# Expert weights of a two-layer transformer step pass through twelve SBUF buffers in place of six

## The reference, cut to what matters

```
glog = x @ w_rg; gsel = argmax(glog)                 # one of 4 groups for each token
elog_g = (x @ w_re) of the group gsel                # 4 experts in a group
top_p, top_i = top_k(softmax(elog_g), 2)             # two experts of the group, renormalised
hid = silu(x @ w_g[e]) * (x @ w_u[e])                # D_EXPERT = 256
y   = sum_e gate[e] * hid[e] @ w_d[e]
```

## Time and profile before

| | |
|---|---|
| median of 3 runs | 1904.09 us (1903.96 to 1904.28) |
| profiled execution, its own time | 1903.26 us |
| its span in the profile | 1901.7 us |
| PE busy | 1690.2 us, 89% of the span |
| DVE, ACT, POOL busy | 1015.7, 874.1, 663.5 us |
| transfers | 360.07 MB, mean 189 GB/s |
| experts of layer 0, from the first split after routing to the last unit's | 714 to 937 us |
| experts of layer 1 | 1648 to 1872 us |

### The profile page before, as it was taken

One profiled execution on the slowest core, in us unless ns is written; L12 is line 12 of the kernel. 1 busy time (PEld: TensorE's weight loads), 2 busy tenths in 40 slices (PEclk: granted clock), 3 DMA queues, 4 the chain that ended last, 5 costly groups with the idle time before them and its releaser, 6 DMA issues. The chain is left out here.

```text
span 1901.7 us, 30317 instructions
## 1 busy us (share of the span) xinstructions
PE 1690.2 (89%) x9817; PEld 1352.0 (71%) x9817; DVE 1015.7 (53%) x1807; ACT 874.1 (46%) x1493; POOL 663.5 (35%) x425
## 2 busy tenths in 40 slices
PE   3799998999999979999739999989999998899994
PEld 2588786776878757777627887867768786677773
DVE  0314437665432158899632263475634502789895
ACT  0343333534443337777513332444444333477773
POOL 1454453333456621000114444533334666101001
PEclk8899999999999989999969999999999999899997
DMA  7622243332556328999872222323344553399994
GB/s 272 221 97 84 91 137 100 106 123 106 184 199 234 111 78 328 374 362 358 313 270 90 89 98 94 128 93 108 114 170 173 208 197 110 128 362 363 362 362 179
DMA packets 117036, 360.07 MB, mean 189 GB/s; under 512 B 11740, under 2 KB 31772, under 8 KB 116896
## 3 DMA queue, kind: packets, MB, share of 16 engines
q1 hardware_dynamic: 92656, 320.23, 46.9%
q0 software_dynamic: 5760, 21.02, 2.9%
q10 hardware_dynamic: 18480, 17.08, 2.8%
HBM read 337.51 MB, written 20.77 MB: 188 GB/s over the span
## 5 line engine op out<-in xcount | busy, mean ns | idle before, releaser
L664 POOL TENSOR_TENSOR wlo<-raw,whi 128x1024 fp32r<-128x1024 f32 x204 | 491.6, 2415 | 621.1 <-ACT whi L810 621.0
L1124 PE MATMUL G<-whi,hhi 128*128 128x512 f32 (+1 forms) x1440 | 580.4, 403 | 21.6 <-ACT pB L899 7.4
L1126 PE MATMUL G<-whi,hlo 128*128 128x512 f32 (+1 forms) x1440 | 560.8, 389 | 0.0
L1125 PE MATMUL G<-wlo,hhi 128*128 128x512 f32 (+1 forms) x1440 | 560.5, 389 | 0.0
L1528 DVE TENSOR_TENSOR wlo<-raw,whi 128x1024 fp32r<-128x1024 f32 x288 | 344.7, 1222 | 44.1 <-ACT whi L818 39.9
L818 ACT ACTIVATE whi<-raw 128x1024 fp32r<-128x1024 f32 x288 | 304.4, 1060 | 91.0 <-PE S L1126 32.8
L1124 PEld LDWEIGHTS G<-whi,hhi 128*128 128x128 f32 x1440 | 273.2, 190 | 100.0 <-DVE wlo L1528 23.8
L1126 PEld LDWEIGHTS G<-whi,hlo 128*128 128x128 f32 x1440 | 272.7, 189 | 58.4
L1125 PEld LDWEIGHTS G<-wlo,hhi 128*128 128x128 f32 x1440 | 273.6, 190 | 48.8
L810 ACT ACTIVATE whi<-raw 128x1024 fp32r<-128x1024 f32 x204 | 213.5, 1054 | 176.4 <-PE G L1126 97.0
L1143 PE MATMUL O<-raw,cond 128*32 128x128 f32 x1536 | 59.7, 320 | 55.1 <-DMA raw<-in_units 45.1
(11 more groups left out here) (301 smaller groups left out, 2190.5 us busy)
## 6 DMA issues: line engine op xcount, KB each, us to landing
raw<-in_units SPq DMA_DIRECT2D x588, 512.0 KB, 5.2
y_sorted<-yo POOLq DMA_DIRECT2D x12, 512.0 KB, 7.1
hs<-h_sorted POOLq DMA_DIRECT2D x10, 514.0 KB, 7.5
bias<-in_nat_bias ACTq DMA_DIRECT2D x16, 256.0 KB, 3.2
h_sorted<-sig POOLq DMA_DIRECT2D x6, 514.0 KB, 13.2
x_scratch<-pA SPq DMA_DIRECT2D x2, 1536.0 KB, 13.1
pA<-x_scratch ACTq DMA_DIRECT2D x2, 1536.0 KB, 9.8
pC<-g_scratch ACTq DMA_DIRECT2D x4, 512.0 KB, 8.4
```

The source lines that it names most:

```text
L664: lo_done.of(nc.gpsimd.tensor_tensor(wlo[:, k, :], raw[:, POS_OF[g] % RAW, :], whi[:, k, :].bitcast(F32), ALU.subtract))
L1124: nc.tensor.matmul(dst, st_hi, mv_hi, start=start, stop=False)
L1125: nc.tensor.matmul(dst, st_hi, mv_lo, start=False, stop=False)
L1126: return nc.tensor.matmul(dst, st_lo, mv_hi, start=False, stop=stop)
```

## The change

The experts' units pass through a ring of twelve buffers (`RING = 2 * RAW`). Six of them are new views of memory that is there already: three of `yacc` and three of `pB` (list `more`). Unit n of a tile goes to buffer n % 12: 0 to 5 are the views, 6 to 11 the six of `raw`. The views have semaphores of their own (`w_more`). ACT and DVE read a unit through `expert_raw(n)`; their order and that of PE and POOL are as before. The loads ahead of the experts are now twelve: units 0 to 2 into `yacc` when the last users of that memory are done, units 6 to 11 into `raw` as it comes free, units 3 to 5 into `pB` after the last transpose of the second norm (`nt_pe`). `load_gate` follows them. From then on SP waits for `e_lo` of unit n and issues unit n+12. The projections' stream keeps its six buffers.

```
+RING = 2 * RAW
...
+        more = [yacc[:, t, :] for t in range(TILES)]
+        more += [pB[:, :, :, :].rearrange("p a t n -> p (a t n)")[:, (1 + i) * D:(2 + i) * D] for i in range(TILES)]
...
+        w_more = [sg(f"w_more{i}", 16) for i in range(RING - RAW)]
...
+        def expert_raw(n):
+            r = n % RING
+            return more[r] if r < RAW else raw[:, r - RAW, :]
...
-                        for r in range(RAW):
-                            released(len(STREAM) - RAW + r)
-                            expert_load(r, 0)
+                        need(kv_out["D"], 1)
+                        sp.wait_ge(*tp_pe.at(l, TP_NO["D", "k", 3]))
+                        sp.wait_ge(*mt_pe.at(l, 3))
+                        for n in range(TILES):
+                            expert_load(n, 0)
+                        for r in range(RAW):
+                            released(len(STREAM) - RAW + r)
+                            expert_load(RAW + r, RAW)
+                        need(nt_pe, 2 * KD - 1)
+                        for n in range(TILES, RAW):
+                            expert_load(n, 0)
                         need(*evacuated(CHUNK_NO["wout", 1], TILES - 1))
                         sp.wait_ge(*g_out.at(l, 1))
                         load_gate(sp, 1)
...
                         with sp.Fori(0, GRP - 1) as i:
                             for k in range(UT // RAW):
-                                next_block(i, k, i * UT + RAW * (k + 1))
+                                next_block(i, k, i * UT + RAW * (k + 2))
...
-                    hi_done.of(nc.scalar.activation(whi[:, n % CONV, :], raw[:, n % RAW, :], ACT.Copy))
+                    hi_done.of(nc.scalar.activation(whi[:, n % CONV, :], expert_raw(n), ACT.Copy))
...
-                    e_lo.of(tt(wlo[:, n % CONV, :], raw[:, n % RAW, :], whi[:, n % CONV, :].bitcast(F32), ALU.subtract))
+                    e_lo.of(tt(wlo[:, n % CONV, :], expert_raw(n), whi[:, n % CONV, :].bitcast(F32), ALU.subtract))
```

More of the change, by code:

```diff
@@ L188 @@
 RAW = 6
+RING = 2 * RAW
 CONV = 3
 NBLOCK = OVER * UT // RAW
-assert UT % RAW == 0 and len(STREAM) % RAW == 0 and NG % CONV == 0 and UT % CONV == 0
+assert UT % RING == 0 and len(STREAM) % RAW == 0 and NG % CONV == 0 and UT % CONV == 0
 POS_OF = [p for p, s in enumerate(STREAM) if s[0] == "gemm"]
@@ L329, in program @@
         gact = sig[:, :, :].rearrange("p t n -> p (t n)")[:, TILES * DEXP:].rearrange("p (t n) -> p t n", t=TILES)
+        more = [yacc[:, t, :] for t in range(TILES)]
+        more += [pB[:, :, :, :].rearrange("p a t n -> p (a t n)")[:, (1 + i) * D:(2 + i) * D] for i in range(TILES)]
+        assert len(more) == RING - RAW
         def row(name, lo=0, hi=None):
@@ L581, in _, with expert_load @@
                     elif s == ("experts",):
-                        def expert_load(r, block):
-                            w_in[r].of(sp.dma_start(
-                                raw[:, r, :], a["units"][bass.ds(block + (l * NU + len(STREAM) + r), 1), :, :]
+                        def expert_load(n, block):
+                            r = n % RING
+                            w = w_more[r] if r < RAW else w_in[r - RAW]
+                            w.of(sp.dma_start(
+                                expert_raw(n), a["units"][bass.ds(block + (l * NU + len(STREAM) + n % RAW), 1), :, :]
                                 .rearrange("a p n -> p (a n)")))
@@ L598, in next_block @@
                         def next_block(i, k, block):
-                            for r in range(RAW):
-                                sp.wait_ge(*e_lo.in_tile(l, i, UT, k * RAW + r))
-                                expert_load(r, block)
+                            for n in range(k * RAW, (k + 1) * RAW):
+                                sp.wait_ge(*e_lo.in_tile(l, i, UT, n))
+                                expert_load(n, block)
                         with sp.Fori(0, GRP - 1) as i:
                             for k in range(UT // RAW):
-                                next_block(i, k, i * UT + RAW * (k + 1))
+                                next_block(i, k, i * UT + RAW * (k + 2))
                         need(gidx_dve, UT // RAW - 1)
-                        for k in range(UT // RAW - 1):
-                            next_block(GRP - 1, k, (GRP - 1) * UT + RAW * (k + 1))
+                        for k in range(UT // RAW - 2):
+                            next_block(GRP - 1, k, (GRP - 1) * UT + RAW * (k + 2))
                         for i in range(GRP, NT):
@@ L611, in _ @@
                                 block = block_at((i - GRP) * (UT // RAW) + k)
-                                if k:
-                                    next_block(i, k - 1, block)
-                                else:
-                                    next_block(i - 1, UT // RAW - 1, block)
-                        for r in range(RAW):
-                            w_in[r].n += (GRP - 2) * (UT // RAW)
+                                if k >= 2:
+                                    next_block(i, k - 2, block)
+                                else:
+                                    next_block(i - 1, UT // RAW - 2 + k, block)
+                        for w in w_in + w_more:
+                            w.n += (GRP - 2) * (UT // RING)
             sp.wait_ge(layer_end.handle, DEPTH + 1)
@@ L812, in high @@
                 def high(i, n):
[L814 to L816 removed]
+                    r = n % RING
+                    w, first = (w_more[r], 0) if r < RAW else (w_in[r - RAW], len(STREAM) // RAW)
+                    act.wait_ge(w.handle, w.value(l, first + n // RING) + i * (16 * (UT // RING)))
                     act.wait_ge(*e_unit.in_tile(l, i, UT, n - CONV))
[L818 removed]
+                    hi_done.of(nc.scalar.activation(whi[:, n % CONV, :], expert_raw(n), ACT.Copy))
                 def rows_high(hf, i):
```

## The result

| | before | after |
|---|---|---|
| median of the runs, same chip | 1904.03 us (4 runs, 1902.29 to 1904.28) | 1884.3 us (4 runs, 1881.35 to 1887.94) |
| ratio, 95% interval | | 0.9919 [0.9894, 0.9943] |
| span of the profiled execution | 1901.7 us | 1886.4 us |
| predicted | | 1891 us, range 1883 to 1898 |

The change makes the kernel faster, by 11 to 20 us of 1904 in this comparison. The ratio is an estimate over all runs with their scatter, not the quotient of the two medians (which is 0.9896 here). Measured again on two other chips the ratio was 0.9931 and 0.9923. So 13 to 15 us is the better figure: single runs of the kernel before lie up to 13 us from their median on those chips, and four runs place a median badly.

The account below looks back on a forecast made before the run. PE was taken to set the pace, with transfers late only at times; 8.5 us in the experts plus 4.5 between the layers, 13.0 off 1903.26, gave 1890.3, plus 0.8 for the runs' median: 1891 us, range 1883 to 1898.

Parts of the forecast that it names:

- the boundary: From layer 0's last expert loads to the layer's end: 3.5 us from the write plus 1.0 from the gather, 4.5 us.
- the DMA row's 9: Profile's DMA share during the experts: looks transfer-bound, but the prediction said transfers have some 10% to spare on average.
- the term 16.1 - 12 x 0.63 = 8.5 us: Experts, both layers: PE's 16.1 us of waits less 0.63 us that stays in each of twelve tiles; gain 8.5 us.
- The bound of 16.1 us: Experts, both layers: the most that better supply could give, if all of PE's waits go.
- The prediction's check of 8.5 us against the tile: Experts: 8.5 us over twelve tiles is 0.7 us each, bringing the mean tile to about 36.6 us.
- I take the whole difference, 3.5 us: End of layer 0: POOL's wait for the last result's write falls from 5.92 us to layer 1's 2.43.
- another 1.0 us: Gather at the end of layer 0: 1.0 us gained of the 3.3 us by which it exceeds layer 1's.
- The bound of 5.1 us: Between the layers: the most to be had, since PE's modulation group ends 5.1 us before DVE's last add.
- All waits gone: Rival: all of PE's waits in the experts and all of the boundary go, 21.2 us, giving 1883 us; chance 0.12.
- Little reaches the end: Rival: supply improves, but DVE's backlog halves the experts' gain or the boundary gives nothing; 1896 to 1900 us, chance 0.15.
- The change doesn't do what it says: Rival: units are late because of when buffers come free, not how many; nothing moves, 1904 us, chance 0.06.
- Slower by a deeper queue: Rival: in each layer's first tile POOL's hs read stands behind more loads, the turn waits 10 us; 1911 us, chance 0.05.

Follow-up runs that it names:

- norows: Kernel before (six buffers) with POOL's row transfers of a tile made small, output not the reference's; ratio 0.9931, median 1886.5 us beside 1899.7.
- ring8: Changed kernel with a ring of eight buffers in place of twelve; ratio to the kernel before 0.9936, median 1885.4 us beside 1897.6.
- nohead: Changed kernel, twelve buffers, but only six loads before the experts begin; ratio to the kernel before 0.9956, median 1889.1 us beside 1897.6.
- swap: Changed kernel with the ring's halves in the other order, units 0 to 5 in the old buffers; ratio to the kernel before 0.9907, median 1883.7 us.
- again2: The changed kernel measured a third time, nothing altered; ratio to the kernel before 0.9923, median 1882.1 us beside 1895.2.
- again: The changed kernel measured once more, nothing altered; ratio to the kernel before 0.9931, median 1884.9 us beside 1897.6.
- jump: Changed kernel, but a layer's last expert load waits for unit 17, not unit 11; ratio to the kernel before 0.9933, median 1883.1 us.
- bparams: Kernel before (six buffers) with SP's layer-end wait moved from the parameters' loads to the copy of x; ratio 0.9975, median 1892.6 us beside 1895.2.

## Why the prediction was right, and where its terms were off

The forecast (1886 to 1896 us, 1891) has the right sign and size: the ratios 0.9919, 0.9931 and 0.9923, applied to 1904, give 1889 to 1891, and the median on the first chip, 1884.3, is within the range of 1883 to 1898, though below the 1886. Two terms were off, in opposite directions: the experts gave 13.8 us where I had 8.5, the boundary 1.9 to 2.8 where I had 4.5. That 1891 came so close is partly luck, since these errors cancel in part, and the stages together (about 16 us) show more than the whole does (13 to 15).

*Cause in the experts: right.* The late units of the earlier trace rows came from POOL's row transfers meeting a ring of six. norows shows it from one side and ring8 and nohead from the other. That the DMA row's 9 is no bound was right as well: from 718 to 752 us, most of the first tile of the changed kernel and the start of the second, the queues moved

```profile
DMA packets 3746, 13.69 MB, mean 403 GB/s; under 512 B 414, under 2 KB 414, under 8 KB 3742
```

where a whole tile of before went at 349 to 373. The 358 GB/s of the Trainium skill (DMA: Bandwidth & Descriptors, section Bandwidth) are passed here too, over 34 us; the same section gives that figure for both cores of an HBM pair streaming at once, and this kernel runs on one core.

*Size in the experts: the term 16.1 - 12 x 0.63 = 8.5 us was undersized; 13.8 measured.* Two parts, which the traces show and no run tested alone. First, what stays is less than 7.6 us: PE's waits are 5.0 us in the 18 places of the four rows above, and ten of these, 3.0 us, are the wait for elo behind the turning of the hidden rows. The gain in waits as shown is 16.1 - 5.0 = 11.1 us. Second, a wait costs more than its row shows. On PE's timeline of the changed kernel:

```profile
853.31 0.39 PE L1146 MATMUL S<-wlo,ehi 128*128 128x512 f32 x1
853.53 0.39 PE L1147 MATMUL S<-whi,elo 128*128 128x512 f32 x1
854.24 0.49 PE L1145 MATMUL S<-whi,ehi 128*128 128x512 f32 x1 [0.32 <-DVE elo L1549]
```

Matmuls follow each other at about 0.23 us, but each is drawn 0.39 us long, since its end is modelled. The third starts 0.71 us behind the second, 0.48 us later than at that pace, and the row shows 0.32. So 0.16 us of each wait is drawn as busy time. Before had 33 such places, after 18: 15 x 0.16 = 2.4 us. 11.1 + 2.4 = 13.5 us, against 13.8 measured. Added up from start to start over these places the delays are 21.2 us before and 7.8 after, which is nearly the same difference. The bound of 16.1 us that I gave for this stretch left that out and should have been 16.1 + 33 x 0.16 = 21.4.

The prediction's check of 8.5 us against the tile hid this. The tile came out as it said, 36.6 us, but the two tiles of the earlier trace rows were short ones: behind the first tile, from fourth unit to fourth unit, the tiles of before took 37.0 to 37.5 us in layer 0 and 37.4 to 38.8 in layer 1.

*First tile.* From its fourth unit to the next tile's it takes 40.4 us before and 37.5 after in layer 0, 39.4 and 37.5 in layer 1. So 4.8 of the 13.8 us are in the two first tiles. The prediction spread the gain evenly over twelve. Without the head start (nohead) they take 41.2 and 39.3 us, so the length of the ring gives nothing there and this share is the head start's.

*Between the layers: 4.5 us predicted.* The order of events came as said: the modulation loads start at 920.00, right behind DVE's split of unit 18 on its timeline,

```profile
918.60 1.22 DVE L1549 TENSOR_TENSOR wlo<-raw,whi 128x1024 fp32r<-128x1024 f32 x1
```

at 918.60 + 1.22 = 919.8. They start 10.7 us ahead of the write, before it was 6.6. The write's wait fell from 5.92 to 3.07 to 3.86 us, where I took 2.4. To the end of the layer 2.4 to 3.2 us were gained, to the copy of x 1.9 to 2.8. So the term was oversized by some 2 us, and its cause is only half right. The failed step is "I take the whole difference, 3.5 us": 2.1 to 2.9 us of it came. The gather, for which I took another 1.0 us, went from 15.8 us behind the write's end to between 14.7 and 16.3 in the three profiles, from 1.1 gained to 0.5 lost. I had added the two as if they were independent. The profiles point to a trade between them. Behind the first six modulation loads four more are issued as PE uses up the first ones, and the earlier they are issued, the longer the gather takes, with small exceptions. No run moved these four alone, so this is a reading and not shown as a cause. The seven kernels with a longer ring and the parameters' wait in place, by the issue of these four against the write and the gather's length, are:

| us | swap | again2 | nohead | ring8 | after | again | jump |
|---|---|---|---|---|---|---|---|
| four loads issued behind the write | 3.6 | 4.2 | 4.2 | 4.3 | 6.9 | 7.2 | 7.9 |
| gather, first issue to last sum | 16.1 | 15.7 | 16.1 | 15.6 | 14.5 | 14.1 | 13.1 |

So the write and the gather together take 19.1 to 21.0 us in them, whatever the order of the loads was.

What stays open is the 22.3 us of the kernel before (22.9 in bparams). It issues the four loads at 7.4, near jump's 7.9, but its gather takes 15.2 us and the whole stretch 2.8 us more than jump's. The two differ in more than the jump's burst, which starts 6.6 and 7.5 us ahead of the write: between 26 and 11 us ahead of the write SP issues ten expert loads in the kernel before and four in jump. Part of the difference can also be scatter, since the gather of equal kernels varied by 1.6 us. No run separates these.

The bound of 5.1 us also moved: PE's second modulation group, which before ended 5.1 us ahead of the layer's end, ends 1.4 us behind it in the changed kernel, at 951.24 against 949.87.

*The rivals.* "All waits gone" (1883) is wrong as a mechanism, since 5.0 us of PE's waits stay, though the first median was near its time. "Little reaches the end": DVE does not bound the tile, which went to 36.66 us with DVE as busy as before (33.88 us). "The change doesn't do what it says": ScalarE's 24.1 us of waits for transfers went to nothing, and the loads that wait for nt_pe came at 688.2, ahead of the 697 that I had named. "Slower by a deeper queue": POOL's read of hs in the first tile of the changed kernel,

```profile
726.34 0.61 POOL L779 DMA_DIRECT2D hs<-h_sorted  x1
739.68 0.71 POOL L768 TENSOR_TENSOR gate<-hs,ones 128x4 f32<-128x4 f32 x1 [12.72 <-PE G L1476]
```

comes 2.0 us earlier than in the earlier trace rows and the turn that lets POOL go on 5.4 us earlier. Five of SP's loads are under way at this read in both kernels, so the pair alone tests little. The prediction said that no row shows two depths side by side; nohead does. At its read,

```profile
729.63 0.61 POOL L779 DMA_DIRECT2D hs<-h_sorted  x1
```

eleven of SP's loads are under way, and it lands 7.25 us later, where the changed kernel's with five under way takes 7.20. In layer 1 it is 7.39 us with eleven and 7.28 with five. A deeper queue of SP didn't hold POOL's reads back.

## What to carry to other kernels

Where an engine waits for transfers though their mean rate is enough, count how much other traffic comes in one piece: here six buffers were enough without the rows, eight with 1 MB of rows a tile, and twelve gave nothing more. Read the price of such waits from start to start of the waiting engine's instructions, since idle time behind a pipelined matmul is drawn too short. At a boundary, look which loads stand behind a wait in program order without needing it; moving that wait past three small loads was worth 6.7 us by the stages and 4 to 6 by the ratios, beside 13 to 15 for the change.

## What the runs showed of the hardware that was not expected

The write of the last result was made 16 times smaller in norows (128 x 64 in place of 128 x 1024), and POOL still waited 4.55 us for it behind the burst of loads; at the end of layer 1, with nothing under way, the same small write took 1.27 us and the whole one 2.43. So behind other loads most of a write's time did not come from its own size.

POOL's read of hs took the same 7.2 to 7.4 us to land with eleven loads of SP under way as with five.

The time of the first stretch varied by 8.4 us of 670 between kernels with the same work in it, and the whole time of the kernel before by up to 13 us around its median (1889.2 to 1910.6, 25 runs). The three runs shown ahead of the prediction lay within 0.3 us of each other (1903.96 to 1904.28), which says little about the spread elsewhere.
